# Prompt attention and linear attention interleaved with the paged stream of a hybrid decoder step

## What is computed

```python
k_past = cache_k[page_table, :, l].reshape(DB, past, DIFF_HEADS, 2 * DIFF_DQK)
v_past = cache_v[page_table, :, l].reshape(DB, past, DIFF_HEADS, DIFF_DV)
o_diff_s = diff_attn_sample(dq, dk, dv, k_past, v_past, lam)
...
o_gla, s_fin = gla_chunked(padf(gq), padf(gk), padf(gv), padf(glog), s0, GLA_CHUNK)
o_diff = diff_attn_prompt(dq, dk, dv, lam)
```

## Time and profile before

| | us |
|---|---|
| median of three runs | 2400.14 (2399.14 to 2403.88) |
| the profiled execution: its time / its span | 2400.51 / 2398.7 |
| project | 0 to 353 |
| linear attention | 357 to 503 |
| sampled linear attention | 503 to 548 |
| prompt attention | 548 to 774 |
| paged attention | 775 to 1507 |
| merge and route, experts, combine | 1507 to 2398.7 |

### The profile page before, as it was taken

The page is one execution under the profiler, slowest core; times in us unless marked ns, Lnnn a source line. Parts: engine busy times, 40 slices in busy tenths (PEclk is TensorE's granted clock), DMA queues, the critical chain, the costliest instruction groups (busy, mean ns, idle before and its releaser), DMA issues. The chain is left out here.

```text
span 2398.7 us, 39482 instructions
## 1 busy us (share of the span) xinstructions
PE 2064.1 (86%) x14525; PEld 1516.4 (63%) x14525; DVE 1262.3 (53%) x1975; ACT 1083.9 (45%) x1919; POOL 406.0 (17%) x370
## 2 busy tenths in 40 slices
PE   6999998987887889889888888699179999999991
PEld 5777776765555566565565555255158888888870
DVE  4313414434665534533533533232478888888874
ACT  4312223312443434434434534322067777878760
POOL 0000000000000333233233232000212221212213
PEclk9999999975688999999999999799579999999995
DMA  5121115010000998998998998341079999999976
GB/s 176 49 76 53 64 51 205 1 27 13 1 1 10 392 406 350 404 371 361 392 381 365 380 392 312 133 176 44 10 288 385 404 405 405 404 403 399 407 296 234
DMA packets 106648, 577.14 MB, mean 241 GB/s; under 512 B 14592, under 2 KB 19840, under 8 KB 53520
## 3 DMA queue, kind: packets, MB, share of 16 engines
q0 software_dynamic: 44448, 293.89, 30.6%
q1 hardware_dynamic: 62064, 281.22, 30.3%
HBM read 531.26 MB, written 43.81 MB: 240 GB/s over the span
## 5 line engine op out<-in xcount | busy, mean ns | idle before, releaser
L1792 DVE TENSOR_TENSOR e_l<-first_w,e_h 128x1024 fp32r<-128x1024 f32 x256 | 294.7, 1218 | 10.1 <-ACT e_h L1789 9.9
L1189 PEld LDWEIGHTS ps<-ident,d_ring 128*128 128x128 f32 x2048 | 236.6, 148 | 97.1 <-ACT d_kT L1252 83.6
L1789 ACT CAST e_h<-first_w 128x1024 fp32r<-128x1024 f32 x256 | 250.3, 1049 | 82.3 <-POOLq L1861 42.7
L1252 ACT COPY d_kT<-ps 128x512 f32<-128x512 f32 x256 | 149.8, 586 | 274.7 <-PE ps L1189 272.2
L1189 PE MATMUL ps<-ident,d_ring 128*128 128x128 f32 x2048 | 263.4, 286 | 9.0 <-DMA d_ring<-in_cache_k,d_row 6.9
L1751 PE MATMUL ps<-e_h,e_xh 128*128 128x512 f32 x512 | 207.1, 404 | 3.6 <-DVE e_xl L1801 3.6
L1753 PE MATMUL ps<-e_h,e_xl 128*128 128x512 f32 x512 | 203.9, 398 | 0.0
L1752 PE MATMUL ps<-e_l,e_xh 128*128 128x512 f32 x512 | 203.9, 398 | 0.0
L1300 DVE COPY d_kT<-ps 128x512 f32<-128x512 f32 x256 | 172.4, 687 | 35.6 <-PE ps L1189 31.9
L1238 PE MATMUL ps<-d_ring,d_pT 128*8 128x128 f32 x4096 | 157.8, 280 | 18.2 <-issue 11.8
L304 PE MATMUL ps<-wh,xh 128*128 128x512 f32 (+1 forms) x432 | 173.4, 401 | 0.0
(11 more groups left out here) (321 smaller groups left out, 3513.5 us busy)
## 6 DMA issues: line engine op xcount, KB each, us to landing
first_w<-in_w_down SPq DMA_DIRECT2D x32, 2048.0 KB, 9.0
first_w<-in_w_up SPq DMA_DIRECT2D x62, 1024.0 KB, 8.8
first_w<-in_w_gate SPq DMA_DIRECT2D x62, 1024.0 KB, 11.3
ys_d<-e_y SPq DMA_DIRECT2D x32, 512.0 KB, 10.1
w<-in_w_in SPq DMA_DIRECT2D x6, 2048.0 KB
ys_d<-cat SPq DMA_DIRECT2D x1, 8192.0 KB, 24.7
kT<-in_x_prompt SPq DMA_DIRECT2D x8, 512.0 KB, 4.5
m_wout<-in_w_out SPq DMA_DIRECT2D x2, 2048.0 KB, 10.7
```

Of the source, the lines that this page charges most:

```text
L1189: mm = pe.transpose(k.ps[:, h, r * P:(r + 1) * P], ring[:, g % RING, r, h * P:(h + 1) * P], ident)
L1789: return act.copy(h13[:, :, kk, :], w13[:, :, kk, :])
L1792: return dve.tensor_tensor(l13[:, :, kk, :], w13[:, :, kk, :], h13[:, :, kk, :].bitcast(F32), ALU.subtract)
```

## The change

One block, `attention`, takes the place of linear attention, sampled linear attention, prompt attention and paged attention. Its order is one list, `SCHEDULE`, that PE, ACT, DVE and SP all follow:

```diff
+LAG = 4
+NT = SAMPLES * GROUPS
+def prompt_phases():
+    order = [("h_decay", 0), ("rest", 0), ("h_turn", 0), ("h_pair", 0), ("h_out", 0), ("h_state", 0), ("rest", 0)]
+    for i in range(TILES):
+        order.append(("g_decay", i))
+        if i:
+            order += [("rest", i), ("rest", i)]
+        order.append(("g_state", i))
+        if i:
+            order += [("g_turn", i), ("g_pair", i), ("g_pair2", i), ("g_out", i)]
+    order.append(("values", 0))
+    for n in range(len(ATT) + 1):
...
+        for j in range(max(scores, outs)):
+            order.append(("a_step", (n, j)))
+    return order
+def schedule():
+    phases, halves = prompt_phases(), 2 * (NT + LAG + 1)
+    order, done = [], 0
+    for x in range(halves):
+        order.append(("sample", (x // 2, x % 2)))
+        if done < len(phases):
+            order.append(phases[done])
+            done += 1
+    return order + phases[done:]
```

The stream has 133 steps of two half steps. Step t transposes and scores key group t and multiplies value group t - 4; the softmax is now a running one over chunks of two groups. There are 171 phases (18 of them empty, `rest`), so they end at step 85. A half step of PE and the phase work that waits most:

```diff
+                def sample(t, half):
+                    if half == 0:
+                        if t < NT:
+                            turn(t, 0)
+                            turn(t, 1)
+                        if 1 <= t <= NT:
+                            scores(t - 1)
+                        if t % 2 == 0 and 0 <= t - LAG < NT:
+                            turn_probs((t - LAG) // 2)
+                    else:
+                        if t < NT:
+                            turn(t, 2)
+                            turn(t, 3)
+                        if 0 <= t - LAG < NT:
+                            values(t - LAG)
...
+                def turn_probs(n):
+                    pe.wait_ge(s_exp, n + 1)
+                    if n:
+                        pe.wait_ge(s_ok, n + 1)
+                    for g in range(2 * GROUP):
+                        mm = pe.matmul(k.ps[:, 3, 32 * g:32 * g + 32], s[:, n % 2, P * g:P * (g + 1)], pick, start=True, stop=True)
...
+                def a_turn(n, j):
+                    if j == 0:
+                        pe.wait_ge(s_p, n + 1)
...
+                def a_step(n, j):
+                    if n and j == 0:
+                        a_weights(n - 1)
+                        a_combine(n - 1)
+                    if n < len(ATT) and j < len(key_parts(ATT[n][0])):
+                        a_maxima(n, j)
```

```diff
-    STORED = [(1, i) for i in range(1, TILES)] + [(2, i) for i in range(TILES)] + [(5, i) for i in range(1, TILES)]
+    STORED = [(0, i) for i in range(TILES)] + [(1, i) for i in range(1, TILES)] + [(2, i) for i in range(TILES)] + [(5, i) for i in range(1, TILES)]
```

More of the change, by code:

```diff
@@ new lines, in _, with turn @@
+                mm.then_inc(s_n5, 1)
+                pe.wait_ge(s_ok, 1)
+                def turn(t, h):
+                    if h == 0:
+                        arrived(pe, "k", t)
+                    if 2 * t + h // 2:
+                        pe.wait_ge(s_ktd if h % 2 else s_kta, 2 * t + h // 2)
+                    x = PLACE[("k", t)] % RING
+                    for r in range(GROUP):
+                        mm = pe.transpose(k.ps[:, h % 2, r * P:(r + 1) * P], ring[:, x, r, h * P:(h + 1) * P], ident)
+                    mm.then_inc(s_t, 1)
@@ new lines, in values @@
+                def values(v):
+                    n = v // 2
+                    pe.wait_ge(s_ptk, n + 1)
+                    arrived(pe, "v", v)
+                    x = PLACE[("v", v)] % RING
+                    for r in range(GROUP):
+                        for h in range(HEADS):
+                            mm = pe.matmul(k.ps[32 * h:32 * h + PICKED, 3, 256:256 + DV], pT[:, n % 2, v % 2, r, h, :],
+                                           ring[:, x, r, h * DV:(h + 1) * DV], start=v % 2 == 0 and r == 0,
+                                           stop=v % 2 == 1 and r == GROUP - 1, skip_group_check=True)
+                    mm.then_inc(s_pv, 1)
@@ L1333, in _ @@
[L1333 to L1336 removed]
+                dve.tensor_copy(rows[:], rows_f).then_inc(s_rows, 1)
+                eight = new_s.rearrange("p (b j) -> p b j", b=SAMPLES)
+                dve.wait_ge(s_n0, 1)
+                chain.link(dve.tensor_tensor(new_s, k.ps[:, 2, 0:256], const(k, "new_mask"), ALU.add))
@@ new lines, in sample @@
+                def sample(t, half):
+                    n, odd = divmod(t - 2, 2)
+                    if half == 0:
+                        if not odd and 0 <= n - LAG // 2 < CHUNKS_N:
+                            update(n - LAG // 2)
+                        if t < NT:
+                            keep(t, 1)
+                        if not odd and 0 <= t - LAG < NT:
+                            keep_probs((t - LAG) // 2)
+                    else:
+                        if t < NT:
+                            keep(t, 3)
+                        if not odd and 0 <= n < CHUNKS_N:
+                            maximum(n)
```

1581 lines of the change are left out of this document (866 added, 715 removed).

## The result

The changed kernel takes 2424.11 us (median of four runs, 2420.78 to 2425.53), the kernel before 2399.64 us (four runs, 2393.85 to 2403.88). The ratio is 1.0102, 95% interval 1.0078 to 1.0126: **1.0% slower**, 24 us. The forecast was 31 us less, so it is off by 56 us, in the direction that the prediction had given 29%. The profiled execution has a time of 2425.5 us and a span of 2423.7.

What follows compares the result with a forecast made beforehand. PE bounds the stretch with phases, DMA the rest: 5.5 + 12.3 + 709 + 38 + 115 + 10 + 209 + 12 = 1111 us against 1154; less 12 for project and merge, 31 us gained: 2369 us, range 2275 to 2480.

Steps and rivals of the forecast that it cites:

- the clock: Stretch with phases: PE keeps the paged stage's granted clock, 0.93 to 0.95, so 674 us of work take 709 us.
- rival B: Prompt attention: granted clock falls; at 0.80 some 2460 us, deciding from 0.91 down; chance 18%.
- PE's work: Stretch with phases: 276 us for phases plus 398 us for the stream at 4.74 us per step, 674 us.
- The waits: New PE waits for DVE and ACT: linear attention 38 us, prompt attention 115, sampled tokens 10; floor half, ceiling double.
- The start of a sequence: First product of sequences 2 to 8: seven PE waits for issue, 47.7 us, taken as gone without the loop.
- D: Rival: the 48 us of a sequence's start stay, or code fetching costs as much; 2417 us, chance 7%.
- A: Rival: DVE and ACT run ahead, PE's holes halve and the clock stays near 1; 2252 to 2287 us, chance 15%.
- Project: ACT's copy of tile 2 waits for the first slot's store behind chunk 1's weights; 9 us, between 0 and 10.
- the new keys' part: Start of the new stretch: lies beside the 12.3 us from first transfer to first transpose, adding nothing.
- The end: Last chunk's softmax, values and result stores before merge; 12 us.
- What would show it: New stretch: PE 85 to 95% busy before step 85, DMA share 1.00 after, named waits at L870, L1058 and ACT.
- Wrong would be: New stretch: mean clock below 0.91, a stream DMA-bound from the start, or PE waits over 250 us in all.

Runs made afterwards that it cites:

- experiment 3: The changed kernel with all phases put ahead of the stream, nothing interleaved; 2585.62 us in one run.
- the control: The changed kernel with 64 empty half steps added behind the first step of each prompt attention pair, the combination still ahead of PE's transposes; 2427.85 us in one run.

## Why the prediction was wrong

**The step that failed** is the clock: it took that of the paged stage and wrote "it is 674 / 0.95 = 709 us". Work is busy time by clock, which came out at 275 us for the phases alone and at 276 for the same work before (experiment 3). The three stretches with phases give 53.1 x 0.68 + 300.9 x 0.96 + 427.8 x 0.85 = 689 us of work, where 674 were forecast, in 782 us of busy time, where the forecast had 709. Of the 73 us between, 15 are more work and 57 a lower clock: 45 of them in prompt attention, 15 in the sampled tokens' part, and linear attention 3 better than assumed. I carried the clock of a dense stage into one that I had myself given a 3 us hole per pair. This is rival B, with its place and its rule: it was to decide "from a clock of 0.91 down", and the mean over 390 to 1298 is 689 / 782 = 0.88. At 18% and a price at 0.80 it was put too low in chance and too high in price; the mild fall that I counted mostly as a gain was enough. The filler and the half steps of their own show that the holes hold the clock down in prompt attention (0.85 with them, 0.97 in both runs); why it is low in the sampled tokens' part, 15 of the 57 us, is open. The 57 us are as much as the whole miss of 56. All else cancels: 15 us of work, 10 of the start, 10 of the end and 1 of merge too little, and 37 us of waits too many (126 us of idle time in the three stretches, where 163 stood). That these came out even is luck.

**PE's work was sized well.** Prompt attention 364 us against 362, sampled tokens 36 against 37, linear attention 289 against 274. The products of L887 take 1.81 us per chunk, not 1.71, and a step 4.9, not 4.74. That PE bounds this part and DMA the rest is shown by the run with half of these products.

**The waits were right in place and count, and smaller than forecast.** At L1058 for DVE's L1507, 32 times: 2.6 us on average and 84.0 in all, where 3.1 stood; with what follows in the next phase 88 us of idle time against 115. In linear attention 33 against 38, per tile two waits of about 2.05 at L870 where one of 4.8 stood. I wrote a PE wait of 3 us into the sum as a price of the order; that it was also the thing to take out, worth 91 us, I did not see, since its second price was missing.

**The start of a sequence** was right: the 47.7 us of the earlier trace rows are gone, and the stream alone takes 643 us. Seven of the 256 loads were in the ring by then, and the other 249 take 635 at the rate assumed. D falls: the largest sum of PE's waits for "issue" in the stretch is 3.3 us in 5 (L856). So does A: the idle time did shrink, but only linear attention ran near the full clock.

**Smaller terms.** Project lost 15 us where 10.5 stood with the barrier: the wait is the one named, at the operation named: ACT waited 10.55 us and PE 9.46 behind it, where 9 stood, and PE's busy time in project grew by 5.7 us as well (339.7 against 334.0, at a clock of 0.97 instead of 0.99). For the 1.5 us of one more barrier the prediction had no row; from project's last product to the next block it is 4.1 us instead of 3.2, so 0.9 more. From the first transfer to the first transpose it is 17.6, not 12.3: I wrote that the new keys' part "lies beside it", but PE's own last products there end it, and the transposes wait for DVE's copy of them (L1302). The end took 15 us from the last landed values to merge, not 12, and the 82 loads 216, not 209. Merge's 3 were 3.8.

**What would show it**, as the prediction listed: the waits at L1058 and L870, the DMA share of 1.00 behind the phases (1.01 over 1298 to 1505, the 0.94 above holds the end) and ACT's wait were all found. PE was 83 to 92% busy before step 85 where 85 to 95 stood. "Wrong would be: a mean clock below 0.91" is what came.

**Where the expected gain went.** The overlap itself is worth 157 us (experiment 3), and the stream by itself is 86 us shorter than the paged attention before (729 against 643): 48 of these are the waits where the loop went round, 18 are seven loads that were in the ring already (7 x 2.55), and the rest was not taken apart. But the phases' own order, which had hidden the chains, was given up in the cutting: alone they cost 632 us instead of 421. Interleaved, most of that hid again beside the stream; what did not hide came back as 84 us of holes at L1058, 33 in linear attention and 57 us of clock, and project added 15. Giving the long chains half steps of their own, with the two stores first, turns the 1.0% loss into a gain of 4.0%.

## What to carry to other kernels

When PE bounds a stretch, forecast its time as work over clock, and take the clock from a stretch with the same holes, not the same instructions; holes of 2.6 us each, 84 in all, came with 45 us of slower clock here, so they cost one and a half times themselves. This is no fixed price: with 92 us of such holes further apart (the control, clock 0.91 over 788 to 1433) it is 549 x (1 - 0.91 / 0.95) = 23 us, an estimate by the same sum. When a chain of another engine is cut into a common order, give its parts slots between two pieces of PE's work and keep the slot in which PE needs the result behind them (the waits of 84.0 us at L1058 became 3.4); then look at how the periods of the two sequences meet, since a shift by two slots cost 14 us (one run), through fewer and longer holes (8 of 4.7 us where 16 of 2 stood). The same instructions took 58.8 us in one program and 67.3 in another (the sampled tokens' part), so do not read a difference of that size from one trace. Keep a store that frees a buffer ahead of a large load in the same queue: ACT's wait for it was 10.55 us behind the load and 3.72 ahead of it.

## What the runs showed of the hardware

Twelve transposes of no use in each of 31 holes made the kernel 34 us faster, by raising the granted clock of prompt attention from 0.85 to 0.97. Fifty-six of them at the start of the stretch did not raise that of the part behind (0.68 with and without them). Products of 64 rows ran at 0.50 to 0.55 with PE busy throughout in three programs and at 0.93 to 1.00 in the changed kernel, though two of the three have the changed kernel's instructions up to there. In linear attention about the same idle time (37 and 33 us) went with a clock of 0.88 in holes of 4.7 us and 0.96 in holes of 2. The same phases ran at 0.50 to 0.72 without the stream between them and at 0.68 to 0.96 with it.
